# Half of the projection back moved into the last delta turn, and normalisation moved behind the attention projections

## What is computed

```python
u = rms_norm(h, norm_g) @ w_in                         # layer A
o, s_new = gated_delta_rule(q, k, v, g, beta, s0)
o = rms_norm(o, out_norm_g) * silu(z)
h = h + o.reshape(B, L, 4096) @ w_out                  # projection back

u = rms_norm(h, kv_norm_g) @ kv_w                      # shared key side
k, v = rms_norm(u[..., :W], k_norm_g), u[..., W:2 * W]
logf = log_sigmoid(u[..., 2 * W:] + f_bias)            # forget gates
f = cumsum(logf)
u = rms_norm(h, norm_g) @ w_in                         # layer B
q, z = rms_norm(u[..., :W], q_norm_g), u[..., W:]
h = h + (softmax(q k^T / sqrt(128) + f_t - f_s) v * silu(z)) @ w_out
```

## Time and profile before

| | us |
|---|---|
| median of three runs | 3677.63 (3671.14 to 3679.14) |
| profiled execution | 3674.46 |
| its span | 3672.7, granted TensorE clock 0.966 |
| PE busy | 3478.3 (95%) |
| DVE busy | 2111.1 (57%) |
| ACT busy | 1503.0 (41%) |
| POOL busy | 774.4 (21%) |

### The profile page before, as it was taken

The page is one execution under the profiler, slowest core; times in us unless marked ns, Lnnn a source line. Parts: engine busy times, 40 slices in busy tenths (PEclk is TensorE's granted clock), DMA queues, the critical chain, the costliest instruction groups (busy, mean ns, idle before and its releaser), DMA issues. The chain is left out here.

```text
span 3672.7 us, 70070 instructions
## 1 busy us (share of the span) xinstructions
PE 3478.3 (95%) x25595; PEld 3324.2 (91%) x25595; DVE 2111.1 (57%) x3455; ACT 1503.0 (41%) x3211; POOL 774.4 (21%) x1050
## 2 busy tenths in 40 slices
PE   5889999999999999999689998799999999999799
PEld 3889999999999999999689997799999999999699
DVE  4556667776676767776232223566666666665422
ACT  4345545555555555555232112333333333333322
POOL 0234555544444455554000000000000000000000
PEclk9899999999999999999799999899999999999899
DMA  3423343343333334433163333333333333332443
GB/s 117 113 78 96 102 106 104 97 109 89 94 106 96 102 105 106 110 89 78 51 183 103 102 106 93 101 97 89 104 97 86 101 97 88 102 94 60 135 123 100
DMA packets 686031, 367.93 MB, mean 100 GB/s; under 512 B 135027, under 2 KB 654054, under 8 KB 685382
## 3 DMA queue, kind: packets, MB, share of 16 engines
q1 hardware_dynamic: 598902, 305.16, 30.6%
q10 hardware_dynamic: 87040, 61.56, 5.6%
HBM read 296.54 MB, written 49.13 MB: 94 GB/s over the span
## 5 line engine op out<-in xcount | busy, mean ns | idle before, releaser
L836 PE MATMUL main<-xh,w_hi 128*128 128x280 f32 x3072 | 713.0, 314 | 14.1 <-DVE w_lo L1073 14.1
L836 PE MATMUL main<-xh,w_lo 128*128 128x280 f32 x3072 | 652.1, 294 | 0.0
L836 PE MATMUL main<-xl,w_hi 128*128 128x280 f32 x3072 | 648.9, 293 | 0.0
L836 PEld LDWEIGHTS main<-xh,w_hi 128*128 128x128 f32 x3072 | 497.8, 191 | 26.9 <-issue 15.0
L836 PEld LDWEIGHTS main<-xh,w_lo 128*128 128x128 f32 x3072 | 493.3, 190 | 0.0
L836 PEld LDWEIGHTS main<-xl,w_hi 128*128 128x128 f32 x3072 | 490.6, 190 | 0.0
L1798 PE MATMUL b_main<-xh_b,b_w_hi 128*128 128x280 f32 x2048 | 471.7, 312 | 12.2 <-DVE b_w_lo L2003 12.2
L1798 PE MATMUL b_main<-xh_b,b_w_lo 128*128 128x280 f32 x2048 | 434.2, 293 | 0.0
L1798 PE MATMUL b_main<-xl_b,b_w_hi 128*128 128x280 f32 x2048 | 432.5, 293 | 0.0
L1798 PEld LDWEIGHTS b_main<-xh_b,b_w_hi 128*128 128x128 f32 x2048 | 327.5, 190 | 23.8 <-issue 12.2
L804 POOL TENSOR_TENSOR Tl<-Tl,prod 40x30 f32<-40x30 f32 (+14 forms) x480 | 330.3, 688 | 37.6
(11 more groups left out here) (276 smaller groups left out, 6111.7 us busy)
## 6 DMA issues: line engine op xcount, KB each, us to landing
w_raw<-in_a_w_in SPq DMA_DIRECT2D x192, 512.0 KB, 4.3
a_w_raw<-in_a_w_out SPq DMA_DIRECT2D x64, 512.0 KB, 4.0
b_w_raw<-in_kv_w SPq DMA_DIRECT2D x64, 512.0 KB, 4.1
b_w_raw<-in_b_w_in SPq DMA_DIRECT2D x64, 512.0 KB, 4.0
y_w_raw<-in_b_w_out SPq DMA_DIRECT2D x32, 512.0 KB, 5.5
kqk<-kq SPq DMA_DIRECT2D x16, 640.0 KB, 4.2
o<-ot ACTq DMA_DIRECT2D x16, 560.0 KB, 6.0
a_o_raw<-o SPq DMA_DIRECT2D x32, 280.0 KB, 3.8
```

What stands on the lines that cost most here:

```text
L836: m = nc.tensor.matmul(main[2 * (t % 2) + h][:, 0:HALF], hi[:, n % SPLIT_RING, k, :], x[:, KSUB * (n % 2) + k, h * HALF:(h + 1) * HALF], s ...
```

## The change

Three things.

1. `last_pair_order` puts the first half of the projection back (heads 0 to 15, 16 k-steps) of the first four output tiles into the last delta turn: 64 `back` k-steps, 384 matmuls (L900 of the new kernel), in place of the dummies. 18 of them stand ahead of `inv5a`, one behind each `seq1` and `seq2`, two behind each `seq3` and `otr`, and the rest at the end. Their weight splits (`b_split`), the splits of 16 o tiles (`o_split`) and the additions of the residual (`b_evac`) run on ACT and DVE; SP and ACT issue the loads, SP stores the sums in the place of h0.
2. `delta_back` replaces `project_back` and the pass over h1: 12 more first-half tiles, then 16 second-half tiles, 28 jobs of 96 matmuls. In the second half h is split un-normalised into attention's input, its squares are added up over the tiles on DVE, and the raw logits are formed on PE. The first two weight steps of each part are prepared by the part before.
3. Attention multiplies by r where a tile leaves PSUM, now on DVE; ACT squares and takes tanh from SBUF. r, log-sigmoid and the cumulative sums are made in the first attention turn (`gates`, at the places in `GATE_PLACES`).

```diff
-BUSY_A, BUSY_B = 6, 3
+BUSY_B = 3
+BACK_TILES = 4
+BACK_FIRST = 18
+BACK_BEHIND = {"seq1": 1, "seq2": 1, "seq3": 2, "otr": 2}
+O_RING = 8
...
+def last_pair_order():
+    left = [("back", j, k) for j in range(2 * BACK_TILES) for k in range(KSUB)]
+    def some(n):
...
+            steps.append(("back", j, k))
+            if k == KSUB - 1:
+                steps.append(("b_split", j + 2))
+                if j % 2:
+                    steps.append(("b_evac", j // 2))
...
+    for j in range(2):
+        steps += [("b_split", j)] + [("o_split", KSUB * j + k) for k in range(KSUB)]
+    steps += some(BACK_FIRST)
+    for s in order.steps:
+        steps += [s] + some(BACK_BEHIND.get(s[0], 0))
+    return Order(steps + some(len(left)), order.ahead, SUBS)
...
@@ delta layer, SP, last turn @@
+                    sp.wait_ge(o_out.sem, 16 * (PAIRS - 2))
...
+                    for k in range(O_RING):
+                        load_o(sp, k)
+                    for j in range(2):
+                        load_back(sp, j)
                     swap(turn)
+                    load_back(sp, 2)
                     lanes_out(turn)
...
@@ delta layer, PE @@
-                    if not turn.front and what in ("inv5a", "inv5b", "seq1", "seq2", "seq3", "otr"):
-                        keep_busy(BUSY_A)
-                    if what == "kstep":
+                    if what == "back":
...
+                        if k == 0:
+                            pe.wait_ge(lo_made, FRONT_SUBS + j + 1)
...
+                        if m == 0:
+                            pe.wait_ge(o_lo, kk + 1)
+                        for hi, x in ((w_hi, xh), (w_hi, xl), (w_lo, xh)):
+                            for h in range(2):
+                                mm = nc.tensor.matmul(main[2 * (m % 2) + h][:, 0:HALF], hi[:, j % SPLIT_RING, k, :],
+                                                      x[:, kk, h * HALF:(h + 1) * HALF],
...
@@ delta layer, ACT (DVE the same with the low parts) @@
+                    if what == "o_split":
+                        act.wait_ge(o_in[k % O_RING], 16 * (k // O_RING + 1))
...
+                        if 1 <= k <= KT - O_RING:
+                            load_o(act, k - 1 + O_RING)
+                    elif what == "b_split":
+                        act.wait_ge(w_in[n % RAW_RING], 16 * (n // RAW_RING + 1))
+                        act.wait_ge(sub_used, n - SPLIT_RING + 1)
...
+                            load_back(act, j + 2)
...
+def delta_back(nc, top, io, keep, scratch):
+    jobs = [(0, m) for m in range(BACK_TILES, KT)] + [(1, m) for m in range(KT)]
...
+                    if j == 0 and i > FIRST:
+                        logit(i - 1)
...
@@ delta_back, ACT, per job @@
+                split(2 * i + 2)
+                if not last:
+                    split(2 * i + 3)
+                for k in o_parts(i):
+                    nc.scalar.activation(oh[:, k], o_raw[:, k % o_ring], ACT.Copy).then_inc(o_hi, 1)
+                act.wait_ge(h_made, i + 1)
+                if half:
+                    nc.scalar.activation(xh[:, m], h[:, i % 2], ACT.Copy).then_inc(x_hi, 1)
+                    nc.scalar.activation(sq[:], h[:, i % 2], ACT.Square).then_inc(squared, 1)
+                act.dma_start(io["h1"][m] if half else scratch["h0"][m], h[:, i % 2]).then_inc(h_out[i % 2], 16)
...
@@ attention @@
+GATE_PLACES = [0.01, 9.01, 13.01, 20.01, 26.02, 34.01]
...
-                            for e in range(2):
-                                if t != 1:
-                                    nc.scalar.activation(sq[:, s], b[e][:, 0:HALF], ACT.Square)
-                                m = nc.scalar.activation(raw[:, t, s], b[e][:, 0:HALF], ACT.Copy)
+                        if t in (0, 2):
+                            wait(act, normed.after(turn, t))
+                            nc.scalar.activation(sq[:], raw[:, t], ACT.Square).then_inc(kept.sem, 1)
+                        elif t == 3:
+                            wait(act, normed.after(turn, t))
+                            nc.scalar.activation(zt[:], znew[:], ACT.Tanh, scale=0.5).then_inc(z_tanh.sem, 1)
...
@@ attention, DVE @@
+                    elif what == "evac":
+                        dve.wait_ge(sub_used, SUBS_B * p + 2 * t + 2)
+                        out = znew if t == 3 else raw[:, t]
+                        for e in range(2):
+                            m = nc.vector.tensor_tensor(out[:, s], b[e][:, 0:HALF], r[:, s], ALU.mult)
+                        m.then_inc(normed.sem, 1)
...
@@ first turn of attention, PE, ahead of the first sum of squares @@
+                        if turn.fixed and p == 0 and t == 0:
+                            pe.wait_ge(g_v, 8)
...
@@ first turn of attention, ACT, ahead of the fetch of FP and FS @@
+                            act.wait_ge(stored, 5 * 16)
```

More of the change, by code:

```diff
@@ L268, in pair_order @@
     return place(places, arguments, SUBS * KSUB, set(list(arguments)[:list(arguments).index("tab")]), SUBS)
+def last_pair_order():
+    left = [("back", j, k) for j in range(2 * BACK_TILES) for k in range(KSUB)]
+    def some(n):
+        steps = []
+        for _ in range(min(n, len(left))):
+            _, j, k = left.pop(0)
+            steps.append(("back", j, k))
[3 more added lines that the diff above has]
+                    steps.append(("b_evac", j // 2))
+        return steps
+    order = pair_order({**PAIR_PLACES, **LAST_PAIR_PLACES})
+    steps = []
+    for j in range(2):
[4 more added lines that the diff above has]
+    return Order(steps + some(len(left)), order.ahead, SUBS)
 def group(g):
@@ L1510, with head_order @@
 }
-def head_order(places):
+GATE_PLACES = [0.01, 9.01, 13.01, 20.01, 26.02, 34.01]
+HANDED = 2
+def head_order(places, gates=()):
     blocks, once = [(i,) for i in range(BLOCKS)], [()]
@@ L1665, in attention_layer @@
+    return place({**places, "gates": list(gates)}, arguments, SUBS_B * KSUB, set(list(arguments)[:list(arguments).index("tab")]), SUBS_B)
 def attention_layer(nc, top, io, keep, scratch):
     order, last_order = head_order(HEAD_PLACES), head_order({**HEAD_PLACES, **LAST_HEAD_PLACES})
+    first_order = head_order(HEAD_PLACES, GATE_PLACES)
     raw_ring, split_ring = 4, 2
@@ L1742, in turns @@
         def turns(engine, body):
-            body(Turn(order, 0, behind=False))
+            body(Turn(first_order, 0, behind=False))
             body(Turn(order, 1))
@@ L1782, in body @@
                 if not turn.front:
-                    wait(pe, kept.after(turn, 2, ago=1))
+                    wait(pe, normed.after(turn, 2, ago=1))
                 for step in turn.steps():
@@ L1791, in body @@
                         if k == 0:
-                            pe.wait_ge(lo_made, SUBS_B * p + n + 1)
+                            if not (turn.fixed and SUBS_B * p + n < HANDED):
+                                pe.wait_ge(lo_made, SUBS_B * p + n + 1 - HANDED)
                             if n % 2 == 0:
-                                wait(pe, (kept.after(turn, 2, ago=1), gate.after(turn, ago=1), kept.after(turn, 0),
-                                          kept.after(turn, 1))[t])
+                                wait(pe, (normed.after(turn, 2, ago=1), normed.after(turn, 3, ago=1), normed.after(turn, 0),
+                                          normed.after(turn, 1))[t])
                         for hi, x in ((w_hi, xh), (w_hi, xl), (w_lo, xh)):
@@ L1803, in body @@
                             m.then_inc(sub_used, 1)
+                    elif what == "gates":
+                        n, = a
+                        if n == 0:
+                            for e in range(2):
+                                m = nc.tensor.matmul(E[e][:, 0:HALF], ones[:, :], acc[:, e * HALF:(e + 1) * HALF], start=True, stop=True)
+                            m.then_inc(g_p, 1)
+                        elif n == 1:
+                            pe.wait_ge(g_a, 1)
+                            for c in range(PAST // P):
+                                m = nc.tensor.transpose(E[c // 4][0:FH, P * (c % 4):P * (c % 4) + P], cl_rows[:, c, :], ident[:, :])
+                            m.then_inc(g_p, 1)
+                        elif n == 4:
+                            pe.wait_ge(g_v, 7)
+                            for i in range(BLOCKS):
+                                nc.tensor.transpose(E[0][0:QN[i], FH * i:FH * i + FH], lf[3][:, Q0[i]:Q0[i] + QN[i]], ident[0:FH, 0:FH])
+                                src = fp[:, Q0[i]:Q0[i] + QN[i]] if i < 5 else fs[:, PAST:PAST + SAMPLE]
+                                m = nc.tensor.transpose(E[1][0:QN[i], FH * i:FH * i + FH], src, ident[0:FH, 0:FH])
+                            m.then_inc(g_p, 1)
                     elif what == "sumsq":
@@ L1993, in body @@
                     what, *a = step
+                    if what in ("scale", "split") and turn.fixed and SUBS_B * p + a[0] < HANDED:
+                        continue
                     if what == "scale":
                         n, = a
```

(10 more changed lines are left out.)

537 lines of the change are left out of this document (352 added, 185 removed).

## The result

The change is faster: 3581.52 us (median of 4 runs, 3576.17 to 3588.26) against 3675.97 in the same comparison; ratio 0.9739, 95% interval 0.9713 to 0.9765. The forecast was 3574, range 3555 to 3607. The profiled execution took 3576.62 us, 97.8 less than the profiled execution before. (The half in the title is the half of the heads, and it moved for four of the 16 output tiles: 384 of the projection's 3072 matmuls.)

What follows compares the result with a forecast made beforehand. PE, busy 95% of the span, was taken as the bound. Last turn and projection save 58 us, the step to attention 49, attention loses 3: 104 off 3674.5 gives 3570.5, 3574 at the median, range 3555 to 3607.

Steps and rivals of the forecast that it cites:

- gap: Between the last delta turn and the projection jobs: 8.2 us instead of 13.40 plus the holes of the start-up.
- its own signs: Among them: attention turns under half a microsecond longer; a steady job over 13.5 us or last turn over 120 refutes it.
- The start of the last turn: Back steps fed by splits of o end near 1761.5, inverse steps need about 5.5 us, first seq2 4 us late.
- Rival (b): Last turn: T tiles wait behind other DMA loads, so the inverse comes 9 us late; 3583 us, chance 0.09.
- The chain: Last turn's nine units: 0.13 us longer each from extra matmuls, five weight splits at 1.25 us; splits with evacuations +8.
- rival (a): Last turn's chain pays in full, 4 us per split, five times, first inverse step 10 us later; 3598 us, chance 0.13.
- The logits: Projection's second-half jobs: a logit pair in 16 of 28, 0.95 us each with the seams, 15.2 us.
- Attention: Multiply by 1/rms moves to DVE, which has room except at the turn boundary: 0.2 us a turn, 3 us lost.
- rival (c): Attention's turn boundary costs 1.5 to 4 us a turn; 3594 to 3631, say 3609 us, chance 0.08.
- Term 2: Projection to attention, 61.2 us before: h1 pass and scans go, about 7 left, gates move into first attention turn; 49 saved.
- (d): Slower than before: weight splits queue behind evacuations on DVE, PE stands still 8.4 us a turn; about 3706 us, chance 0.03.
- (e): Better: chain splits hidden, logits at 0.6 us, gates without a wait, no boundary loss; 3554 us, chance 0.04.

Runs made afterwards that it cites:

- narrow run: Against the changed kernel, DVE makes only the first of 560 columns of each low part of the 16 o tiles in the last turn: 3585.76 us.
- second trace of the change: The changed kernel run again unaltered: 3584.83 us.
- deferred run: Against the changed kernel, last-turn weight splits moved: ACT's half behind the next seq3, DVE's half and residual addition behind the following seq1: 3576.74 us.
- run with dummies: Against the changed kernel, no back steps in the last delta turn, and six dummy matmuls ahead of each chain step: 3626.07 us.

## Why the prediction was right, and where it was off

The time, the range and the side came out; several terms of the sum were mis-sized. By its steps, in us, with the trace of the change:

| step | forecast | measured |
|---|---|---|
| last turn up to the first seq2 | 29.3 | 32.5 |
| first seq2 to last otr (53.5 before) | 63 | 64.5 |
| whole last turn | 95 | 99.8 |
| gap | 8.2 | 7.5 |
| 28 jobs with logits and cold start | 362.6 | 367.1 |
| last matmul to attention | 7 | 8.4 |
| gates in the first attention turn | 5 | 4.6 |
| 15 attention turns, added | 3 | 10.1 |

Nearly all misses go one way. The stages from the last turn to the 15th attention turn save 88 us (102.8 - 4.6 - 10.1) where the forecast had 104. The medians differ by 94.5, so some 6 us came from stretches that the forecast says nothing of, and that the median lies only 7.5 us above the forecast is in part luck. Two of its own signs did not hold: a steady job longer than 13.5 us was to make it wrong, and a job with a logit pair takes 13.59; attention turns were to be under half a microsecond longer, and they are 0.67 longer. Both are terms that were mis-sized, as shown below.

**The start of the last turn.** It said: the back steps end near 23.8 us behind the turn (they ended 24.6 behind it), and the inverse steps follow at once. But PE waited 0.96 us for T1s, which came at 25.55, and needed 7.0 us from there to the first seq2 instead of 5.5, with 1.48 us of waiting for TTs. The forecast took POOL's chain as untouched; DVE's splits slowed it by 7 us, and 2.7 came behind it: a longer last step on POOL (2.89 us instead of 2.46), and 4.8 us from the issue of the T1s loads (1751.68) to the step instead of 2.5. The Trainium skill has the rule that the forecast left out (SBUF — State Buffer, Who interferes with whom): a VectorE instruction with two inputs in SBUF contends with a GpSimd instruction that reads SBUF. The trace agrees, 0.93 us against 0.47 for the same step on POOL, and 2.83 against 0.74 on DVE.

**Rival (b)** was not a rival but part of the outcome. Its sign, T tiles later than 1757 on the clock of before, was there (15.7 became 25.6 us behind the turn). In the narrow run, with POOL's chain back at its old pace, they still landed about 22.4 us behind the turn, so the queue alone is enough for the sign. That agrees with the rule of ring order quoted there from the Trainium skill (DMA: Bandwidth & Descriptors, Queues, rings and completion order): a store issued behind the loads took 9.6 us until the load that waits for it went out, instead of at most 2.9. Its price of 9 us was wrong: the back steps cover all but the 0.96 us of PE's wait for T1s and a part of the wait for TTs, and in the second trace of the change PE does not wait for T1s at all, since the back steps themselves end at 27.9.

**The chain.** The sum was near (64.5 for 63) by two errors that offset each other. The leg behind seq3 was put at 0.13 a unit; twelve matmuls and seq3 itself bind PE there, and it grew by 0.47 and the unit by 0.37, with the otr units 4.8 us in all instead of 1.2. Splits and residual were put at 8 (five times 1.25 and six times 0.44 are 8.9; the sum is 0.9 short); they cost 6.1, and by their place alone, as the deferred run shows. A split in a unit cost 1.1 us, so rival (a), 4 us a split, did not come.

**The logits** were mis-sized: 0.95 us a pair with the seam, measured 1.25. I read the row of four matmuls as two pairs; the trace shows each float32 matmul of the code as two, so the row is one pair, and its 1.12 us lie above the bound of 1.0 that the forecast set. Fifteen pairs stand within the jobs (the last one follows them): 15 x 1.25 = 18.8 instead of 15.2 are 3.6 of the 4.5 us by which the jobs are long. The other 0.9 lies in the cold start, the seams and small steps, which were not taken apart.

**Attention.** Work on DVE and the boundary were seen rightly, 0.2 a turn, but the loss was 0.67, still below the 1.5 at which rival (c) begins, and most of it at another place: not the last evacuation but the first, which stands one place ahead of a step that empties a bank for PE. The forecast went through the waits at the boundary only, because there the engines were late before; what had been on time with nothing ahead of it was not looked at.

**Term 2** held: the pass over h1 went, 8.4 us are left, and the gates cost 4.6 us of the first turn.

**Rivals (d) and (e)** did not come. The forecast's chief claim, that 49.3 us of matmuls cost the turn some 15 and save some 34, is borne out by the run with dummies: 13.4 and 35. The 66.9 us of the rest are read from the windows and were not tried one by one.

## What to carry to other kernels

When independent matmuls are put into the holes of a dependent chain, their own preparation (splits, evacuations) stands in the in-order queues of the chain: place each where that engine waits anyway, not where the piece of work happens to end. When an operation is moved to another engine, go through every step that follows it there and ask who waits for it, above all those that empty a bank. And a filler of dummies may already pay for itself by the clock, so the new work is to be weighed against dummies, not against an idle engine.

## What was not expected of the hardware

- Without filler PE ran the whole chain at a granted clock of 0.50, and a unit took 6.17 us; 34 times six dummy matmuls brought it to 0.97 and 4.90. The last turn with 384 useful matmuls is only 5 us longer to the first job than with none (107.3 against 102.6).
- A step of POOL's took 0.93 instead of 0.47 us beside DVE's subtractions of two SBUF tiles, and such a subtraction 2.83 instead of 0.74 us beside POOL's last step.
- With the DMA share above 1 (264 GB/s) a store of 160 KB issued on SP at 1754.12 was usable only at 1763.75, more than 6 us longer than the 2.9 us of before.
- The end of turn 15, with the same code, moved by up to 18 us between executions, at a mean granted clock of 0.97 to 0.98.
